# Low parts of the gather rows made by TensorE and ScalarE, shared products moved behind the first gate-up, and unread products in TensorE's waits, in a two-layer decoder with mixture of experts

## The reference: what is computed

```
h = rms_norm(x, norm1_g) * (1 + scale1) + shift1
x = x + gate1 * attention(h)          # layer 0 dilated, layer 1 latent (MLA) on shared keys and values
h = rms_norm(x, norm2_g) * (1 + scale2) + shift2
x = x + gate2 * moe_ffn(h)
```

## Time and profile before

| | |
|---|---|
| median of three runs | 1295.28 us (1295.25 to 1299.4) |
| the profiled execution, its own time | 1298.68 us |
| its span | 1296.9 us |
| TensorE busy, mean granted clock | 1098.4 us (85%), 0.941 |
| VectorE busy | 495.6 us (38%) |
| ScalarE busy | 249.6 us (19%) |
| read from HBM | 500.04 MB, 386 GB/s over the span |
| chain that ended last | SyncE's queue 52%, TensorE 31%, DMA 7%, VectorE 5% |

### The profile page before, as it was taken

The page is one execution under the profiler, slowest core; times in us unless marked ns, Lnnn a source line. Parts: engine busy times, 40 slices in busy tenths (PEclk is TensorE's granted clock), DMA queues, the critical chain, the costliest instruction groups (busy, mean ns, idle before and its releaser), DMA issues.

```text
span 1296.9 us, 17378 instructions
## 1 busy us (share of the span) xinstructions
PE 1098.4 (85%) x6680; PEld 610.0 (47%) x6680; DVE 495.6 (38%) x1108; ACT 249.6 (19%) x574; POOL 0.4 (0%) x5
## 2 busy tenths in 40 slices
PE   5999899998788798787859999999878878878785
PEld 4887477454234234243327577745423433423332
DVE  1297774432313132212227877543231313221231
ACT  2021623111101011111112482311110101111110
POOL 0000000000000000000000000000000000000000
PEclk9999899999799889899989999999988999889998
DMA  9999987999999999999989757799999999999996
GB/s 348 378 402 409 361 321 309 381 423 421 425 424 423 423 423 424 423 423 424 423 314 391 312 196 264 286 379 424 422 424 423 423 423 424 423 423 423 425 423 278
DMA packets 101337, 502.25 MB, mean 387 GB/s; under 512 B 12009, under 2 KB 37510, under 8 KB 46982
## 3 DMA queue, kind: packets, MB, share of 16 engines
q1 hardware_dynamic: 100790, 500.92, 95.1%
q10 hardware_dynamic: 464, 0.20, 0.1%
HBM read 500.04 MB, written 1.05 MB: 386 GB/s over the span
## 4 chain that ended last, share of the span: by engine, by line
SPq 52%; PE 31%; DMA 7%; DVE 5%; issue 4%; ACT 1%; DVEq 0%; ACTq 0%
SPq L585 45%; PE bank L739 23%; SPq L684 3%; DMA ring<-in_moe_w_down 3%; SPq L592 3%; PE bank L1177 2%; PE bank L742 2%; DMA ring<-in_moe_w_gate_up 2%; PE bank L841 1%; PE bank L983 1%; DMA w_gu<-in_ada_w 1%; DMA ring<-in_ada_w 1%; DVE w_dn L1627 1%; PE bank L1158 1%; PE bank L906 1%
## 5 line engine op out<-in xcount | busy, mean ns | idle before, releaser
L739 PE MATMUL bank<-w_gu,ring 128*32 128x512 f32 (+1 forms) x1120 | 296.1, 700 | 109.8 <-DMA w_gu<-in_moe_w_gate_up 35.7
L739 PEld LDWEIGHTS bank<-w_gu,ring 128*32 128x32 f32 (+1 forms) x1120 | 78.7, 132 | 277.9 <-issue 277.6
L1844 DVE TENSOR_TENSOR hh<-sg,bank 128x256 f32<-128x256 f32 x44 | 27.4, 623 | 414.4 <-ACT sg L1445 414.4
L739 PE MATMUL bank<-w_gu_x,ring 128*32 128x512 f32 (+1 forms) x352 | 160.1, 666 | 8.4 <-DMA ring<-in_moe_w_gate_up 5.8
L739 PE MATMUL bank<-ring 128*32 128x512 f32 (+1 forms) x272 | 142.9, 675 | 9.9 <-DMA gate<-in_moe_w_gate_up 5.3
L739 PE MATMUL bank<-w_gu,hhT 128*32 128x512 f32 (+1 forms) x416 | 138.3, 596 | 9.4 <-DMA ring<-in_moe_w_down 7.6
L739 PE MATMUL bank<-w_dn,ring 128*32 128x512 f32 x240 | 118.3, 795 | 8.0 <-DMA w_gu_x<-in_moe_w_gate_up 8.0
L1445 ACT ACTIVATE sg<-bank 128x256 f32<-128x256 f32 x44 | 16.9, 384 | 497.9 <-PE bank L739 497.9
L1861 DVE SCALAR_TENSOR_TENSOR bank<-bank,w_slot,gate 128x512 f32<-128x512 f32 x88 | 66.8, 759 | 103.7 <-PE bank L739 103.7
L739 PE MATMUL bank<-ring,hhT 128*32 128x512 f32 (+1 forms) x208 | 87.4, 596 | 1.2 <-DVE hhT L1851 0.6
L739 PE MATMUL bank<-sel,h_hi 128*128 128x256 f32 x352 | 87.8, 290 | 0.0
(11 more groups left out here) (299 smaller groups left out, 1687.6 us busy)
## 6 DMA issues: line engine op xcount, KB each, us to landing
w_gu<-in_moe_w_gate_up SPq DMA_DIRECT2D x130, 1024.0 KB, 25.6
w_gu<-in_moe_w_down SPq DMA_DIRECT2D x46, 1024.0 KB, 26.4
w_gu_x<-in_moe_w_gate_up SPq DMA_DIRECT2D x40, 1024.0 KB, 26.0
ring<-in_ada_w SPq DMA_DIRECT2D x36, 1024.0 KB, 10.1
ring<-in_moe_w_gate_up SPq DMA_DIRECT2D x34, 1024.0 KB, 26.3
w_dn<-in_moe_w_gate_up SPq DMA_DIRECT2D x28, 1024.0 KB, 26.2
ring<-in_moe_w_down SPq DMA_DIRECT2D x22, 1024.0 KB, 26.3
w_dn<-in_moe_w_down SPq DMA_DIRECT2D x14, 1024.0 KB, 26.0
```

The lines of the kernel that those rows point to most:

```text
L739: return nc.tensor.matmul(o, a, b, start=first, stop=last)
L1844: v.tensor_tensor(hh[:, :].rearrange("s (f p) -> s p f", f=FE // P), sg[:, :].rearrange("s (p f) -> s p f", f=FE // P), bank[b][:, FE:2 * ...
```

## The change

- Norms 1, 2 and 3: VectorE scales x into `xn` in two halves of 512 columns, and TensorE transposes `xn` instead of multiplying x by `diag_r`. Norm 2 makes the shared keys' input first.
- Head of the experts: TensorE's transposes write the banks in the order in which the gather rows lie, ScalarE copies `h_hi`, TensorE subtracts it in the bank (a product with minus identity, `low_part`), and ScalarE copies the rest as `h_lo`. VectorE's four subtractions are gone. Of the 16 products of `shared_gate_up(0, ..)` six stand ahead of `chosen`, the other ten now stand behind the first `gate_up`. ScalarE's `sh_g` goes behind `silu(0)`. In layer 1 the two products of `gate_half(3, ..)` move from norm 3 to behind the first `gate_up` as well.
- Attention of layer 0: `ada_steps(6, ..)` one turn later (turns 3 to 6), `ada_columns(6)` in turn 7; ScalarE takes a turn's exponentials before its copies. In layer 1 ScalarE's order is as it was.
- `fill`: products whose results nobody reads: 12 + 5 + 3 at the start, 2 + 1 at norms 1 and 3, 8 + 2 at norm 2.
- `block_sums`: 8 products of 512 columns for 16 of 256.

```diff
         def interleaved(h, j):
-            return h[:, j // 2, :, :].rearrange("t k (c q) -> t c q k", c=KT)[:, 4 * (j % 2):4 * (j % 2) + 4, :, :]
+            return h[:, j // 2, :, 64 * (j % 2):64 * (j % 2) + 64]
...
+            def fill(n, w=None, b=5):
+                w = cst if w is None else w
+                for _ in range(n):
+                    mm(bank[b][:, 0:N], w[:, 0:P], w[:, 0:N], True, True)
...
             def norm_transposes(n):
-                pe.wait_ge(sem("xn_ready"), 2 * n + 2)
+                fill(8 if n == 2 else 1)
                 for j in range(4):
+                    if j % 2 == 0:
+                        pe.wait_ge(sem("xn_ready"), 2 * n + 1 + j // 2)
...
-                            last = mm(bank[j][:, kk * N + ti * P:kk * N + (ti + 1) * P], x[:, ti, k * P:(k + 1) * P],
-                                      diag_r[:, ti, :], True, True)
+                            last = tr(bank[j][:, kk * N + ti * P:kk * N + (ti + 1) * P], xn[:, ti, k * P:(k + 1) * P])
...
-                if n == 3:
-                    gate_half(3, 0)
-                    gate_half(3, 1, 6)
...
+                def low_part(j):
+                    pe.wait_ge(sem("h_act"), 8 * l + j + 1)
+                    nc.tensor.matmul(bank[j][:, :], neg_ident[:, :], interleaved(h_hi, j), start=False,
+                                     stop=True, skip_group_check=True).then_inc(sem("h_ps"), 1)
...
-                shared_gate_up(0, 0, 6)
+                shared_gate_up(0, 0, 6, 0, 2)
+                pe.wait_ge(sem("routing"), 2 * l + 1)
+                for j in range(4):
+                    low_part(j)
+                    shared_gate_up(0, 0, 6, j + 2, j + 3)
                 pe.wait_ge(sem("chosen"), l + 1)
...
-                shared_gate_up(0, 1, 6)
...
-                pe.wait_ge(sem("h_act"), 4 * l + 4)
-                pe.wait_ge(sem("h_dve"), 4 * l + 4)
+                pe.wait_ge(sem("h_act"), 8 * l + 8)
                 gather_half(0, 0)
                 gather_half(0, 1, (2, 3))
...
                 gate_up(0)
+                if l == 1:
+                    gate_half(3, 0)
+                    gate_half(3, 1, 4)
+                shared_gate_up(0, 0, 6, 6, KT)
+                shared_gate_up(0, 1, 6)
+                pe.wait_ge(sem("tables_sb"), 3 * l + FLAGS_SB)
```

More of the change, by code:

```diff
@@ L913, in experts, with shared_gate_up @@
                     for k in range(4):
-                        last = tr(bank[j][:, k * P:(k + 1) * P], hT[:, 4 * half + k, ti * P:(ti + 1) * P])
+                        last = nc.tensor.matmul(turned_rows(j, k), hT[:, 4 * half + k, ti * P:(ti + 1) * P], const("ident"),
+                                                start=k == 0, stop=True, is_transpose=True, skip_group_check=True)
                     last.then_inc(sem("h_ps"), 1)
-                def shared_gate_up(j, f, b):
+                def shared_gate_up(j, f, b, k0=0, k1=KT):
                     w = use(("sgu", l, j))
-                    for k in range(KT):
+                    for k in range(k0, k1):
                         last = mm(bank[b][:, f * N:(f + 1) * N], w[:, k, f * P:(f + 1) * P], hT[:, k, :], k == 0, k == KT - 1)
@@ L1154, in block_sums @@
                 pe.wait_ge(sem(f"ada_0_in{j}"), 32)
[L1155 to L1160, removed]
+                for k in range(2):
+                    for q in range(4):
+                        last = nc.tensor.matmul(bank[7][32 * q:32 * q + 1, :], csilu[:, 2 * q + k:2 * q + k + 1],
+                                                ada_0[j][:, 2 * q + k, :, :].rearrange("p s n -> p (s n)"), start=k == 0,
+                                                stop=k == 1, skip_group_check=True)
                 last.then_inc(sem("ada_0_used"), 1)
@@ L1423, in attention, with turned, output @@
                             last.then_inc(sem("p_ready"), 1)
+                def turned(g):
+                    if 2 <= g < H // 2 + 2:
+                        if g >= 4:
+                            act.wait_ge(sem("o_ps"), pairs + g - 3)
+                        for h in (2 * g - 4, 2 * g - 3):
+                            act.wait_ge(sem("pT_ps"), heads + h + 1)
+                            copy(pT_sb[:, h % 4, :], bank[4 + h % 2][:, 0:SC]).then_inc(sem("pT_sb"), 1)
+                def output(g):
+                    if g >= 3:
+                        act.wait_ge(sem("o_ps"), pairs + g - 2)
+                        copy(hT[:, g - 3, :], bank[6][:, 0:N]).then_inc(sem("o_sb"), 1)
+                for g in range(H // 2 + 3):
+                    if l == 0 and g == 7:
+                        ada_rows(6)
+                    if l == 1 and g == 2:
+                        for half in range(2):
+                            act.wait_ge(sem("gate_ps"), 4 + half + 1)
+                            copy(gate[:, 0, half * 512:(half + 1) * 512], bank[6 + half][:, :]).then_inc(sem("gate_sb"), 1)
+                    if l == 1:
+                        turned(g)
+                        output(g)
+                        exponentials(g)
+                    else:
+                        exponentials(g)
+                        turned(g)
+                        output(g)
                 root_table(l)
@@ L1697, in attention @@
                             .then_inc(sem("s_ready"), 2)
+                    if g == 7 and l == 0:
+                        modulation(6, 4, 104, col("kv_norm_g", 0, 8))
                     if g >= 1:
```

109 lines of the change are left out of this document (53 added, 56 removed).

## The result

The changed kernel takes 1305.01 us (median of 5 runs, 1304.71 to 1306.63); the kernel before took 1296.45 us beside it (5 runs, 1295.25 to 1299.4). The ratio is 1.0056, 95% interval 1.0036 to 1.0077: slower by about 7 us. The forecast was 1294.8 us within 1287 to 1301. The profiled execution has a span of 1303.0 us against 1296.9.

A forecast was written before the change was run, and what follows sets the result against it. In the expert passes DMA bytes set the time, so only idle DMA ahead of them counts. Layer 0 gains 5.0 us (10.7 - 5.7), layer 1 loses 4.5, so 0.5 us less: 1294.8 us, within 1287 to 1301.

The forecast's parts named there:

- The mechanism of the queue: Head of the experts: SyncE's in-order queue holds later loads behind unit 14's, which goes 12.3 us later against the router.
- D0: Layer 0: time the front gains by the new issue of unit 14's load, 4.2 + 3.4 + 3.1 = 10.7 us.
- the start, 4.2 us: Start of layer 0: fills bring the clock up by 12.69 us, second sums at 20.7 instead of 24.95 us; bounds 0 and 4.3.
- attention, 3.4 us: Layer 0's attention: modulation steps a turn later save a wait and cold products, 3.4 us; bounds 1 and 5.5.
- T + 1.6 - 211.5: Layer 0: DMA idle time ahead of the passes, T being unit 14's new issue time, forecast 216.6 us; 11.7 us before.
- the forecast's formula: Expert heads: gain is 221.6 - T in layer 0, 13.5 + 825.4 - 1.6 - T in layer 1; T: unit 14's issue.
- The rival for this place: Layer 0's attention: the moved turn brings nothing, the wait only moves to another engine; 3.4 us less gain, 1298.2 us, chance 0.11.
- Norm 1, 3.1 us: Layer 0's norm 1: router ends 6.4 us behind the scaling factors, a gain of 3.1 us; bounds 1.5 and 4.
- The rival of the clock falling in the norms: Norms: router at half clock, 3.6 us more in each layer, 6.7 us slower, 1302.0 us; chance 0.06.
- Layer 1: Layer 1: norm 3 gains 3.2 us, less 7.7, so a gain of -4.5 us; bounds -7 to -3.5.
- The base: Whole kernel: the profiled execution, 1298.68 us, lies 3.4 us above the median of the runs, from which the forecast is taken.
- The rival that TensorE's path counts: Up to 281 us: TensorE sets the end, unit 14's delay is covered; 7.9 us faster, 1287.4 us, chance 0.17.

The follow-up runs named there:

- products back: The changed kernel with the ten shared gate-up products put back ahead of the gather, behind `ranks`: 1298.3 us, ratio 1.0007 to the kernel before.
- the second experiment: The kernel before with only the second block of eight shared gate-up products moved behind the first gate-up, `sh_g` behind the first silu: 1318.93 us, ratio 1.017.
- the norms alone: The kernel before with the changed norms 1 to 3 and their own filling products (2 + 1 and 8 + 2): 1293.49 us, ratio 0.9966.
- third experiment: The changed kernel with unit 14's load moved behind the first five loads of the passes in SyncE's list: 1299.08 us, ratio 1.0013 to the kernel before.
- the last kernel above: The changed kernel with the ten shared products ahead of the gather and ScalarE's order in layer 0's attention put back: 1294.83 us, ratio 0.9969 to the kernel before.
- the second set: Comparisons on one chip: changed kernel again 1.0078, layer 0's attention put back 1.0075, only ScalarE's order put back 1.0064, start's fills in the kernel before 1.0004.

## Why the prediction was wrong

The mechanism of the queue was right, and the step that failed is the sum for D0, the time that the front of layer 0 gains: 10.7 us forecast, 227.3 - 223.05 = 4.2 us measured. Two of its three terms were too large: the start, 4.2 us, of which 1.6 reached attention, and attention, 3.4 us, of which 0.3 came.

- **The queue.** From `chosen` to unit 14 it took 17.9 us (205.16 to 223.05), forecast 17.5. The loads follow at once, the dips at 250 and 866 us are gone (DMA share 1.01 from 242 to 252 and from 862 to 872 us), and the DMA stands still ahead: T + 1.6 - 211.5 gives 13.2 us for layer 0 with the measured T of 223.05, and the window above gives 13.3. By the forecast's formula, with this T, layer 0 should lose 1.5 us. The passes of layer 0 end 1.1 us late, layer 1's unit loads come 0.9 us late, and by its formula, counted from there, layer 1 should lose 5.2 us: 0.9 + 5.2 = 6.1, and the span grew by 6.1. Three experiments (products back, load later, products moved in the kernel before) show it, each from another side.
- **Start, 4.2 us.** Measured 3.6 us at 56 us, and 1.6 us at attention. The forecast carried a gain on TensorE through a stretch in which the DMA had none to give. The slices of the kernel before had it, 402 and 409 GB/s from 65 to 130 us, and the forecast didn't use them. Besides, the start's clock is not the same in every execution. Four profiles have the old start: the Q products are cold in three (3.39 us, 3.54 without the fills, 3.56 with the norms alone) and take 1.99 us in the second experiment's. Alone, the fills bring nothing measurable.
- **Attention, 3.4 us.** Measured 0.3 us (unit loads behind the output projection 1.94 us earlier, 1.64 of them from the start). Two things were wrong. First, ScalarE's new order made a wait of 2.47 us a turn later; the prediction counted that order only for the row in turn 7. Second, the 3.4 us were read from an execution in which this stretch was slow. The first pair of steps, cold for 2.75 us there, takes 1.90 us in the five other profiles with the old order, as here in the second experiment's:

```profile
131.18 1.90 PE L739 MATMUL bank<-ring,csilu 128*1 128x512 f32 x16 [1.18 <-issue]
```

  From the first scores to the unit loads behind the output projection, the six profiles with the old order take 65.7 to 68.8 us, and 68.8 is the kernel before's; the five with the changed order take 68.5 to 69.8 us. So no gain is seen; on the mean of these profiles the changed order is 1.8 us slower (69.0 against 67.2). The rival for this place (nothing comes of it) was the right one, at 0.11.
- **Norm 1, 3.1 us.** Measured 2.7 us at `chosen` beyond the 1.94. The factors were ready at 192.91 us and the router ended at 199.7: 6.8 us against 6.4. Right, and borne out by the norms with their filling products. The four subtracting products cost nothing, as forecast: from the router's end to `chosen` it is 5.45 us in both kernels. The rival of the clock falling in the norms is refuted for this kernel: 1.00 from 195 to 199 us. By the rule of the Trainium skill (TensorE: Matmul & The Clock Gate, Part 4: PE-mode transpose) it should have been down if transposes count for nothing; here each norm's transposes last only 1.97 us, between products, and no run has longer ones, so its rule is neither shown nor refuted.
- **Layer 1.** -4.5 us forecast; measured -5.2 us (unit 14 at 842.5 us, if the 0.9 us are taken off by which layer 1 began late, against 841.8). Right within its bounds. Norm 2 brought 0.4 us (1.1 us late ahead of it, 0.75 behind), nearly nothing, as forecast.
- **The base.** The forecast took 3.4 us off the profiled execution to come to the median of three runs. Beside the changed kernel the median of the kernel before was 1296.45 us, 1.2 us more, and in the later sets 1297.5 to 1298.5. So the three runs were low, and 1.2 us of the miss of 10.2 us come from there; in the ratio it plays no part.
- **The rival that TensorE's path counts** fell for the delay (the second experiment). But half of it is true: once unit 14 is early, TensorE's slots at 248 to 252 us set the rest, and loads that start 11 us earlier bring 3 to 4 us a layer (third experiment). That fits the norms' gain coming back nearly in full.

The experiments form a chain, in which each kernel differs from the next by one part or a few. By the ratios: norms and fills -6.5 us; from there to the last kernel above (the rest of the head, the step moved in attention) +2.5; ScalarE's order +4.9 (3.5 by the medians, 1.8 by the ratios of the second set); the shared products behind the gate-up +6.4 to +9.2. That these add up to the 7.3 to 10.1 us measured follows from the chain and confirms nothing; what they show is which links are large. Not settled: what ScalarE's order costs by itself, and why undoing all of attention's change gained nothing.

## What to carry to other kernels

When work is moved behind other work on one engine, look up which buffer its last instruction frees, and what is queued in order behind the load for it. A gain on an engine does not pass through a stretch in which the DMA is full; follow it from stretch to stretch, and carry on only what the slowest one lets through. And if a profile shows a cold or slow stretch, compare it with other executions before you count its end as a gain: both terms that failed here, the start and attention, were read in part from one execution that was slow there.

## What the hardware showed that was not expected

- A wait of 3.35 us of TensorE ahead of the gather was followed by 6 us at a granted clock of 0.50, 2.8 us lost, where the products that used to stand there take 3.7 us and the clock stays at 1.00.
- The start's clock comes up at different times in the same program: the Q products took 3.39 us in one execution and 1.99 us in another with nothing changed ahead of them, the second experiment's. In both the first sums were slow (3.59 and 3.39 us):

```profile
19.71 1.99 PE L1177 MATMUL bank<-w_gu,hT 128*128 128x256 f32 x8 [1.56 <-DVE hT L1937]
```

  The runs of the kernel before spread over 9 us (1293.3 to 1302.5). Twelve runs of it with the start's fills spread over 3.5 us, but six of another kernel with fills, the one with ScalarE's order put back, over 7.8 us. So it is not shown that the fills narrow the spread.
- The old attention took 65.7 to 68.8 us in six executions, from its first scores to the unit loads. In the one that took 65.7 us, with the norms alone, the granted clock was 1.00 from 150 to 160 us; in one that took 68.8, with norms and fills, it was 0.50 from 150 to 155 and 0.83 from 155 to 160 us.
